# Gathered keys and values stored from SBUF in a two-layer hybrid decoder step, with parameters, states and q, k, v weights loaded in another order

## The reference, cut to what matters

```python
proj = rms_norm(x, norm_g) @ w_in        # a_val a_glu a_gate | b_val b_gate | q k v c_gate
u = a_val * sigmoid(a_glu)               # A: causal depthwise conv of width 31, layer norm, swish, gate
pb = pool_buf ++ b_val                   # B: trailing means over 2/4/8/16, a small map, gate
q, k = rope(rms_norm(q)), rope(rms_norm(k))
kk, vv = cache_k ++ k, cache_v ++ v      # C: keys at distances 0..128, 0..512 step 4, 0..2048 step 16
yc = dilated_attend(q, kk, vv) * silu(c_gate)
new_k, new_v = kk[:, -2048:], vv[:, -2048:]
x = x + concat(ya, yb, yc) @ w_out
```

## Time and profile before

| what | value |
|---|---|
| median of 3 runs | 415.51 us (415.07 to 419.36) |
| profiled execution, its own time | 418.61 us |
| its span, first to last instruction | 416.8 us |
| mean granted TensorE clock | 0.95 |
| TensorE, VectorE, ScalarE, GpSimd busy | 84%, 56%, 24%, 11% |
| DMA packets, bytes, mean | 50676, 158.06 MB, 379 GB/s |
| share of q0 (GpSimd), q1 (SyncE), q10 (ScalarE) of 16 engines' span | 59.3%, 25.6%, 14.3% |

### The profile page before, as it was taken

How to read it: one execution, slowest core, us unless ns; L and a number is a source line. 1 busy time by engine, 2 the same in 40 slices (tenths; PEclk the granted TensorE clock), 3 DMA queues, 4 the chain that set the end, 5 groups by cost and what they waited for, 6 DMA issues and landing times.

```text
span 416.8 us, 4509 instructions
## 1 busy us (share of the span) xinstructions
PE 351.3 (84%) x1536; PEld 270.5 (65%) x1536; DVE 232.5 (56%) x522; ACT 99.3 (24%) x234; POOL 46.2 (11%) x87
## 2 busy tenths in 40 slices
PE   1489799977489979999979999997578969999980
PEld 1378688865367756558868888885356755558860
DVE  0334679749974776430123589849986786331010
ACT  3110014530152422410120021641233422310110
POOL 2300011111101111110100001112010111210000
PEclk9999999996878999999998999998969998999996
DMA  8999999999999999999999999999999999999972
GB/s 288 418 418 418 420 414 370 387 401 390 404 411 418 411 383 411 396 373 362 413 392 416 406 361 402 387 403 393 374 411 415 414 369 403 351 339 338 324 282 84
DMA packets 50676, 158.06 MB, mean 379 GB/s; under 512 B 4724, under 2 KB 20030, under 8 KB 49870
## 3 DMA queue, kind: packets, MB, share of 16 engines
q0 software_dynamic: 21824, 95.11, 59.3%
q1 hardware_dynamic: 19652, 39.36, 25.6%
q10 hardware_dynamic: 9178, 23.31, 14.3%
HBM read 149.39 MB, written 104.42 MB: 609 GB/s over the span
## 4 chain that ended last, share of the span: by engine, by line
SPq 38%; DMA 21%; PE 20%; DVE 16%; issue 2%; ACT 1%; ACTq 0%; DVEq 0%
SPq L380 15%; DMA kv<-in_cache_k_win 13%; DMA out<-kv 8%; PE pj L731 7%; SPq L405 6%; SPq L452 5%; SPq L435 5%; PE pj L592 4%; DVE kv L1096 4%; DVE ssc L1099 4%; PE psc L663 3%; DVE yc L1156 3%; SPq L391 3%; SPq L395 2%; PE ptr L508 2%
## 5 line engine op out<-in xcount | busy, mean ns | idle before, releaser
L592 PE MATMUL pj<-hT,w 128*128 128x264 f32 x800 | 195.6, 403 | 8.6 <-DVE hT L1018 6.0
L592 PEld LDWEIGHTS pj<-hT,w 128*128 128x128 f32 x800 | 157.8, 200 | 40.8 <-issue 10.1
L1156 DVE SCALAR_TENSOR_TENSOR yc<-u_ext,par,yc 128x256 f32<-128x256 f32 x180 | 76.2, 481 | 2.8 <-DVE u_smp L1046 0.6
L731 PE MATMUL pj<-mix,w 128*128 128x264 f32 x256 | 59.5, 387 | 0.0
L731 PEld LDWEIGHTS pj<-mix,w 128*128 128x128 f32 x256 | 48.0, 190 | 8.0
L496 POOL DMA_DIRECT2D out<-in_cache_v_win x48 | 25.8, 543 | 180.2 <-issue 180.2
L1226 DVE TENSOR_TENSOR xT<-xT,pj 128x264 f32<-128x264 f32 x16 | 6.9, 429 | 52.9 <-PE pj L731 52.9
L496 POOL DMA_DIRECT2D out<-in_cache_k_win x32 | 18.6, 584 | 138.4 <-issue 131.3
L840 ACT ACTIVATE ex<-pj 128x264 f32<-128x264 f32 x22 | 8.6, 391 | 82.1 <-PE pj L592 66.3
L663 PE MATMUL psc<-kv,spm 128*48 128x384 f32 x80 | 27.5, 496 | 0.0
L1096 DVE TENSOR_TENSOR kv<-kv,qb 128x1536 f32<-128x1536 f32 x10 | 17.6, 1759 | 10.3 <-DMA kv<-in_cache_k_win 10.0
(11 more groups left out here) (172 smaller groups left out, 322.9 us busy)
## 6 DMA issues: line engine op xcount, KB each, us to landing
out<-in_cache_k_win POOLq DMA_DIRECT2D x32, 1512.0 KB, 75.2
out<-in_cache_v_win POOLq DMA_DIRECT2D x16, 1152.0 KB, 75.4
out<-in_cache_v_win POOLq DMA_DIRECT2D x17, 1080.0 KB, 72.9
w<-in_w_out ACTq DMA_DIRECT2D x2, 4096.0 KB, 28.9
out<-in_cache_v_win POOLq DMA_DIRECT2D x16, 432.0 KB, 73.2
w<-in_w_in SPq DMA_DIRECT2D x2, 3072.0 KB, 32.4
w<-in_w_in ACTq DMA_DIRECT2D x1, 4608.0 KB, 30.7
kv<-in_cache_k_win SPq DMA_DIRECT2D x32, 144.0 KB, 25.1
```

Source lines behind the costliest of these rows:

```text
L592: last = nc.tensor.matmul(pj[n % RING][:, 0:T], wbuf[buf][:, k, col:col + P], hT[:, k, :], start=(k == 0), stop=(k == KD - 1))
L731: last = nc.tensor.matmul(pj[n % RING][:, 0:T], w1[:, k, m * P:(m + 1) * P], mix[:, k, :], start=(k == 0), stop=(k == KD - 1))
L1156: last = V.scalar_tensor_tensor(out=yc[:, t, 0:SEQ], in0=x_w, scalar=par[:, ROW_CW + w * CT + t:ROW_CW + w * CT + t + 1], in1=yc[:, t, 0:S ...
```

## The change

- Keys and the far values are stored from `kv` too. `put_back(kind, l, g)` takes one span; the far span's first row would fall before row 0, so it stores 15 of 16 partitions and then, in two more DMAs, the rest of each sample's first partition. SyncE does it for the keys after the b weights, each span once it has landed, and for the values where it did before.
- GpSimd's copies leave out the gathered rows for keys and values alike: pieces of 3 rows, five of each 16 rows in the far span and one of each 4 in the mid span. The three copies of the last rows are gone.
- The product of keys and query goes to `tok4` (of which `v_tok` and `k_tok` are now halves), not back to `kv`. VectorE waits in layer 1 for the stores of `v_tok` and `k_tok`, ScalarE before `vtok` for the last `ks_used`.
- VectorE waits for each span of keys before the first cut that uses it. The value gathers of a span wait for `ks_used` and for that span's key stores. The key gathers of layer 1 wait for that span's value stores.
- conv_w's 93 rows are loaded as 80 and 13 (`row_cuts`).
- Layer 0's conv and pool states are issued once x is in; its q, k, v weights go on SyncE's queue behind a_gate's, with no wait; ScalarE's waits for `squared` and `a_val_in` are gone.
- VectorE copies three of x's transposed pieces before it makes `diagonal`.
- Before y is written to `x_tok`, only the near value stores are waited for.

```diff
+SPAN_AT = [sum(n for _, _, n in GATHER[:g]) for g in range(len(GATHER))]
+FIRST_CUT = [next(i for i, (a, b) in enumerate(SCORE_CUTS) if b > at) for at in SPAN_AT]
+LAST_CUT = [next(i for i, (a, b) in enumerate(SCORE_CUTS) if b >= at + g[2]) for at, g in zip(SPAN_AT, GATHER)]
...
-COPIES = [("k", s, a, a + HALF_ROWS) for s in range(NS) for a in (0, HALF_ROWS)]
-COPIES += [("v", s, a, b) for s in range(NS) for a, b in ((0, 768), (768, EVEN_ROWS), (FAR_LO, GATHER[0][0]))]
+COPIES = [(kind, s, a, b, d) for kind in "kv" for s in range(NS) for a, b, d in
+          ((0, GATHER[1][0] // 2, GATHER[2][1]), (GATHER[1][0] // 2, GATHER[1][0], GATHER[2][1]),
+           (GATHER[1][0], GATHER[0][0], GATHER[1][1]))]
+SPANS = ("near", "mid", "far")
...
+def row_cuts(n):
+
+    even = n // 16 * 16
+    return [(a, b) for a, b in ((0, even), (even, n)) if b > a]
...
-        v_tok = sb("v_tok", [P, 2, C_ATT])
-        k_tok = sb("k_tok", [P, 2, C_ATT])
+        tok4 = sb("tok4", [P, 4, C_ATT])
+        v_tok, k_tok = tok4[:, 0:2, :], tok4[:, 2:4, :]
...
+            def gather(kind, l, g, name):
+
+                (lo, d, n), at = GATHER[g], SPAN_AT[g]
+                for s in SAMPLE_ORDER:
+                    rows = one(f"cache_{kind}_win", l)[:, s, lo:lo + d * n * PER_S]
+                    rows = rows.rearrange("o (a b e) h d -> (o a) b e (h d)", a=PER_S, e=d)[:, :, 0, :]
+                    sp.dma_start(kv[sample_rows(s), at:at + n, :], rows).then_inc(S[name], 16)
+
+            def put_back(kind, l, g):
+
+                name = f"{kind}_{SPANS[g]}_out"
+                out = {"k": o_k_s, "v": o_v_s}[kind][bass.ds(l, 1)]
+                (lo, d, n), at = GATHER[g], SPAN_AT[g]
+                skip = 1 if lo == 0 else 0
+                for s in SAMPLE_ORDER:
+                    r = sample_rows(s)
+                    rows = out[:, s, lo - 1 + d * n * skip:lo - 1 + d * n * PER_S]
+                    rows = rows.rearrange("o (a b e) h d -> (o a) b e (h d)", b=n, e=d)[:, :, 0, :]
+                    sp.dma_start(rows, kv[r.start + 2 * skip:r.stop:2, at:at + n, :]).then_inc(S[name], 16)
+                if skip:
+                    for r in range(2):
+                        rows = out[:, r:NS:2, d - 1:d * n - 1]
+                        rows = rows.rearrange("o s (b e) h d -> (o s) b e (h d)", e=d)[:, :, 0, :]
+                        sp.dma_start(rows, kv[r:P:2 * PER_S, at + 1:at + n, :]).then_inc(S[name], 16)
...
@@ SyncE
                     weights(l, w0, 2 * C_CONV, "w_in", COL["a_gate"], C_CONV, "a_gate_in")
+                    weights(l, w1, 0, "w_in", COL["q"], 3 * C_ATT, "q_in")
...
-                    for name in ("v_near_out", "v_far_out"):
-                        sp.wait_ge(S[name], nth(l - 1, name, per[name]))
-                gather("k", l, "k_in")
+                for g, span in enumerate(SPANS):
+                    if l > 0:
+                        sp.wait_ge(S[f"v_{span}_out"], nth(l - 1, f"v_{span}_out", per[f"v_{span}_out"]))
+                    gather("k", l, g, f"k_{span}_in")
                 if l > 0:
                     sp.wait_ge(S["pj_full"], nth(l - 1, "pj_full", NPROJ))
                 weights(l, w2, 0, "w_in", COL["b_val"], 2 * C_POOL, "b_in")
-                gather("v", l, "v_in", "ks_used")
+                for g, span in enumerate(SPANS):
+                    sp.wait_ge(S[f"k_{span}_in"], nth(l, f"k_{span}_in", per[f"k_{span}_in"]))
+                    put_back("k", l, g)
+                for g, span in enumerate(SPANS):
+                    sp.wait_ge(S["ks_used"], nth(l, "ks_used", LAST_CUT[g] + 1))
+                    sp.wait_ge(S[f"k_{span}_out"], nth(l, f"k_{span}_out", per[f"k_{span}_out"]))
+                    gather("v", l, g, "v_in")
...
@@ ScalarE
             act.wait_ge(x_in, 32)
+            act.dma_start(st_conv[:, :, :], ins["state_conv"][bass.ds(0, 1)].rearrange("o (r s) w c -> (o s w) r c", r=2)
+                          ).then_inc(S["st_in"], 16)
+            act.dma_start(st_pool[:, :], ins["state_pool"][bass.ds(0, 1)].rearrange("o s w c -> (o s w) c")).then_inc(S["st_in"], 16)
             act.wait_ge(early_in, 16)
...
-            act.wait_ge(squared, 1)
...
-            act.wait_ge(S["a_val_in"], 16)
-            weights(0, w1, 0, "w_in", COL["q"], 3 * C_ATT, "q_in")
...
+                        if step == ("vtok", 0):
+                            act.wait_ge(S["ks_used"], nth(l, "ks_used", len(SCORE_CUTS)))
...
@@ VectorE
                         if i == 0:
-                            dve.wait_ge(S["k_in"], nth(l, "k_in", per["k_in"]))
+                            if l > 0:
+                                dve.wait_ge(S["v_out"], l * per["v_out"])
+                                dve.wait_ge(S["k_out"], l * per["k_out"])
                             dve.wait_ge(S["tr_free"], nth(l, "tr_free", TR["qb"] + 1))
-                        V.tensor_tensor(kv[:, a:b, :], kv[:, a:b, :], qb[:, None, :].to_broadcast([P, b - a, C_ATT]),
+                        for g, span in enumerate(SPANS):
+                            if FIRST_CUT[g] == i:
+                                dve.wait_ge(S[f"k_{span}_in"], nth(l, f"k_{span}_in", per[f"k_{span}_in"]))
+                        V.tensor_tensor(tok4[:, :, :], kv[:, a:b, :], qb[:, None, :].to_broadcast([P, b - a, C_ATT]),
                                         ALU.mult).then_inc(S["kprod_ok"], 1)
```

More of the change, by code:

```diff
@@ L368, in one @@
                 return ins[name][bass.ds(l, 1)]
-            def gather(kind, l, name, used=None):
-                at = 0
-                for lo, d, n in GATHER:
-                    if used is not None:
-                        last = next(i for i, (a, b) in enumerate(SCORE_CUTS) if b >= at + n)
-                        sp.wait_ge(S[used], nth(l, used, last + 1))
-                    for s in SAMPLE_ORDER:
-                        rows = one(f"cache_{kind}_win", l)[:, s, lo:lo + d * n * PER_S]
-                        rows = rows.rearrange("o (a b e) h d -> (o a) b e (h d)", a=PER_S, e=d)[:, :, 0, :]
-                        sp.dma_start(kv[sample_rows(s), at:at + n, :], rows).then_inc(S[name], 16)
-                    at += n
@@ L404, in params @@
                     src = one(name, l).rearrange(pat, c=P)
-                    sp.dma_start(prow[r0:r0 + src.shape[0], :], src).then_inc(S["par_in"], 16)
+                    for a, b in row_cuts(src.shape[0]):
+                        sp.dma_start(prow[r0 + a:r0 + b, :], src[a:b]).then_inc(S["par_in"], 16)
                 for r0, name in ((ROW_QN, "q_norm_g"), (ROW_KN, "k_norm_g")):
@@ L460, in _ @@
                 sp.wait_ge(S["v_in"], nth(l, "v_in", per["v_in"]))
-                put_back_values(l)
+                for g in range(len(SPANS)):
+                    put_back("v", l, g)
             y_rows = y_prompt.rearrange("b (r p) d -> r p (b d)", p=P)
@@ L758, in _ @@
                 src = ins[name][bass.ds(0, 1)].rearrange(pat, c=P)
-                act.dma_start(prow[r0:r0 + src.shape[0], :], src).then_inc(S["par_in"], 16)
+                for a, b in row_cuts(src.shape[0]):
+                    act.dma_start(prow[r0 + a:r0 + b, :], src[a:b]).then_inc(S["par_in"], 16)
             for r0, name in ((ROW_QN, "q_norm_g"), (ROW_KN, "k_norm_g")):
@@ L956, in _ @@
                             act.wait_ge(S["xsq"], nth(l, "xsq", KD))
-            for name in ("v_near_out", "v_far_out"):
-                act.wait_ge(S[name], DEPTH * per[name])
+            act.wait_ge(S["v_near_out"], DEPTH * per["v_near_out"])
             act.wait_ge(y_turned, 1)
@@ L976, in _ @@
             dve.wait_ge(zeroed, 1)
[L977 to L983 removed]
+            for u in range(XROUNDS):
+                if u == 3:
+                    dve.wait_ge(early_in, 16)
+                    dve.wait_ge(squared, 1)
+                    for r in range(2):
+                        V.tensor_scalar(diagonal[:, r * P:(r + 1) * P], C["ident"], x_sum[:, r:r + 1], None, ALU.mult)
+                    V.tensor_scalar(diagonal[0:NS, SEQ:T], C["ident"][0:NS, 0:NS], x_sum[0:NS, 2:3], None, ALU.mult)\
+                        .then_inc(diagonal_ok, 1)
+                    dve.wait_ge(diagonal_ok, 1)
                 dve.wait_ge(x_turned, u + 1)
@@ L1229, in _ @@
                 assert chain[0] == DVE_LINKS, chain[0]
-            for name in ("v_near_out", "v_far_out"):
-                dve.wait_ge(S[name], DEPTH * per[name])
+            dve.wait_ge(S["v_near_out"], DEPTH * per["v_near_out"])
             dve.wait_ge(y_turned, 2)
```

53 lines of the change are left out of this document (10 added, 43 removed).

## The result

The changed kernel takes 464.98 us (median of 4 runs, 464.25 to 465.63); the kernel before, on the same chip, 417.28 (415.07 to 419.36). The ratio is 1.114, with a 95% interval of 1.107 to 1.122: slower by 47 us. The profiled execution has a span of 463.8 us against 416.8.

What follows compares the result with a forecast made beforehand. It saw TensorE's matmul chain (84% busy) and the DMA transfers (379 GB/s) both close to a bound. Terms +41 + 2 - 7 + 3 = +39 on the 415.5 us median gave 454 us, 80% range 430 to 470.

Steps and rivals of the forecast that it cites:

- Start: Layer 0's start: first projection about 20.8 us, not 22.26; a_gate's wait of 2.59 goes, new q-weight wait of 7; net +3.
- Keys: Layer 0's gathered keys: VectorE's wait of 5.97 us goes, worth 4; net -1 to the end of the scores.
- Layer 0's values: TensorE at layer 0's value products stands from 156 to 198 us for gathered values landing at 197: +41 (+33 to +45).
- Layer 1's values: Layer 1's value products: values land at about 390 us, TensorE comes at 386 and waits 4; +2 over layer 0's shift.
- End: Kernel's tail after the last y's issue: some 3 us instead of 10, with copies over by 370; -7.
- TensorE's clock: Matmuls after two long stands run at the lower granted clock (1.2 GHz level): +3 us (between 2 and 7).
- Parameter rows, waits added to VectorE and ScalarE: 93 parameter rows loaded as 80 + 13, VectorE's layer 1 wait for stores, ScalarE's for the last `ks_used`: 0 each.
- Nothing: Rival, 4%: gain of keys and end cancels a short wait, or stores leave the DRAM copies no smaller; 415 us.
- Faster: Rival, 7%: far stores are cheap, turns do not pile up, layer 0's values come before 156; 407 us.
- Half: Rival, 13%: q1's short rows pass faster beside fewer copies, completions cost nothing; values in at 180, +24; 431 to 437 us.
- Worse: Rival, 10%: engines with more rows lag and it adds up, or layer 1's wait is 20, not 4; 470 to 480.
- The estimate of 458: Sum if 15-partition far stores use 15 engines and 4-row stores 4: each far store ends about 2.5 us later.

## Why the prediction was right, step by step

Predicted were 454 us (430 to 470) and slower; measured 464.98, inside the range. The mechanism was the one predicted; the terms:

- **Start.** First projection at 20.8: 20.60. It now waits for its own weights (7.65 us), so no more was to be had there from ScalarE. The wait for a_gate gone: gone. A new wait of 7 for q weights landed at about 62: 7.70, at 63.25. Right.
- **Keys.** No wait of VectorE, worth 4, TensorE at the values at about 156: no wait, 157.0. The start's +3 and the keys' -4 were to give -1; they gave 0. The products into `tok4` take 1.76 us, as predicted.
- **Layer 0's values**, the large term: +41 (33 to 45) predicted, landing at 197 (189 to 201); measured +46.7, at 203.7, beyond both bounds. The counting by turns was right: taking 2040 packets out gives 31.0 us (15.2 ns each), 1040 give 13.9 and 888 give 11.6 (13.4 and 13.1 ns). What q10 takes was near too. From 104 us to 160 q1 passed 2733 packets (856 + 1057 + 820); at the prediction's own rates (61 per us for b weights, 39 for near rows, 65.6 for the rest) they are some 45 us' worth of 56, which leaves 11 for q10 where 12 were allowed. The term without a place in the sum is the gap between the engines: 390 packets of the weights behind the gathers pass in the 15.7 us before the last gathered row, 6 us of q1's time at its 62 packets per us. Had the engines finished together, the values would have been in at about 197 (an estimate from these counts), the time predicted. That 197 was met so closely is partly luck: it is a choice between 189 and 201.
- **Layer 1's values.** A wait of 4: 7.8. Landing at 390: 400.4. The copies were to end at 366, by 56 packets per us: 19639 of 19968 were over at 366, and the rest dragged on until 386, 188 of them from 371 on, some 12 per us. The size that was off is the 68 us of remaining work that were to shrink to 24, as rows alone go two to three times as fast. They do where the engines are busy (702 packets from 392 to 396, 175 per us), but from 366 to 400 q1 passed 3385, 100 per us, since the engines did not stay full. The windows (us, busy by engine, granted clock, DMA share, GB/s):

```profile
385.00:390.00 5.00, 2.03 (x9) 1.51 (x9) 2.80 (x9) 1.50 (x6) 0.00 (x0) 0.95 0.76 244
390.00:395.00 5.00, 2.56 (x14) 1.63 (x12) 3.12 (x6) 2.15 (x2) 0.00 (x0) 0.71 0.66 201
395.00:400.00 5.00, 0.00 (x0) 0.00 (x0) 3.98 (x14) 0.00 (x0) 0.00 (x0) 0.63 0.54 156
```

  With the engines full those 15 us would have been 9.8 (0.65 of them, an estimate). Against the predicted arrival at 386 and landing at 390, TensorE arrived at 392.6 and waited 3.8 us longer than the 4 predicted.
- **End.** -7: -7.5 (2.4 for 9.9).
- **TensorE's clock.** +3 (2 to 7). The window over the stand has a granted clock of 0.53, the 1.2 GHz level; it was idle in it:

```profile
155.00:205.00 50.00, 3.30 (x16) 2.05 (x16) 7.10 (x20) 2.15 (x2) 9.40 (x16) 0.53 1.02 383
```

  After it 16 value products took 7.74 us, and 6.69 after layer 1's stand, where the next 16 took 5.36: +3.7 from these two. Right.
- **Parameter rows, waits added to VectorE and ScalarE:** 0, and no wait on the page or in the lists names them.

In sum 39 was predicted and 47 measured: 5.7 more is layer 0's term, 2.8 the way from there to the last y (7.0 + 0.8 measured, 2 + 3 for the clock predicted; layer 1's longer wait is in it), and -0.5 the end's. The other 2.5 us between 454.5 and 465.0: the prediction took the median to be 3.1 below the profiled execution, as in the runs of before that it had; here the profiled execution took 465.63, and the median is 0.65 below it.

**The rivals.** Nothing and Faster fell with the wait at L670. Half fell too: the values landed at 203.7 and not at 180, and completions are not free, since some 400 of q1's 2472 packets from 160 to 200 us are completions (packets of 4 B) and the count still equals q0's 2471. Worse had two conditions. Its wait of 20 in layer 1 did not come in the changed kernel. Its other, engines that lag over the far stores, did come in part: without the far key stores the gap in layer 0 is 6.7 us and not 15.7. It was worth less than 470 to 480 needs; the whole gap is some 6 us of the landing, in the changed kernel, and 4.5 without the far key stores (estimates from the packets that pass in it). In layer 1 the gap is as visible without far key stores as with them, so there they are not shown to be its cause.

The estimate of 458 for it goes by the Trainium skill's "DMA: Bandwidth & Descriptors", "Why a DMA increments its semaphore by 16 and not by 1". By that rule a far store of 15 partitions has 15 completions and one of 4 rows has 4. By it the trace agrees: of the 888 packets a layer that go with the far key stores 760 are rows, so 128 are completions, 8 x 15 + 2 x 4, where the prediction counted 160. Which engines take the rows no row of a trace names, and the 2.5 us for each far store are not isolated by a run; the far key stores' packets together gave back 11.6 us, less than the 13.5 of their number.

The same page of the Trainium skill, section "Queues, rings and completion order", says that an engine round-robins between the queues that have work, a packet at a time. By that rule the trace agrees: 1083, 1073 and 1057 packets, and 2471 and 2472. (A packet of that section is some 9 to 17 descriptors; the profile counts each row as one, and equal counts do not tell how many go in one turn.) The Trainium skill's section "Rules for kernel authors" on that page says that spreading DMAs over SyncE, ScalarE and GpSimd does not help bandwidth and only saves issue time. Here the trace says more: key stores moved from q1 to q10 took 44 to 47 us of value waits from layer 0, at the same bytes, because they no longer stood ahead of the gathers in one queue.

## What to carry to other kernels

Count, for each transfer that an engine waits for, the packets that stand ahead of it in its own queue, and price them by the turns of the queues that run beside it; bytes and DRAM traffic can stay equal or fall, as here, while the critical gather comes 47 us later. That price holds while the queues beside it stay busy; count also the bytes that all queues move before the gather, which set it in layer 1. A gather has landed when the slowest engine is through with it, here 16 us after the first engine had gone on to the next transfer. Data that nobody waits for belongs in a queue where nothing urgent stands behind it, issued by an engine that can stand. And when a wait is taken away upstream, look at the next landing that is fixed by transfers: with a margin near 0 there (1 us here), the gain comes back as a wait.

## What was not expected of the hardware

- The engines do not finish together: before layer 0's values land, packets of the next transfer pass for 15.7 us (2.2 before); the DMA share falls from 0.76 to 0.54 over the last 15 us before layer 1's values land; and without the far key stores some 7 us pass with one or two engines of 16 at work. Stores of 15 partitions and of 4 rows widen the gap in layer 0; what else makes an engine lag stays open.
- Once the copies are over and values are gathered by one queue alone, 156 to 201 GB/s are moved, at DMA shares of 0.54 to 0.66 (the windows above), less than half of the 418 of a mixed slice. Divided by the share that is some 290 to 305 GB/s with all engines busy (an estimate).
- A far store of 15 partitions leaves 15 completions and one of 4 rows leaves 4, not 16 (888 packets a layer).
- A bound on the copies' pieces of 1536 B in place of 4608 B changed neither their number nor their bytes (19968, 84.94 MB).
- An issue of a small DMA stands for the large ones ahead of it in its queue: 12.69 us for two stores of 6 KB, 1.17 with the queue free.
